# Grouped-query attention in a three-block network: the order of scores, turns, exponents and division on three engines

## The reference

```
def block_attention(q, k, v):
    ...
    scale = HEAD_DIM ** -0.5
    def attend(qblk):
        s = jnp.einsum('bqkgd,bskd->bkgqs', qblk, k, preferred_element_type=jnp.float32) * scale
        p = jax.nn.softmax(s, axis=-1).astype(v.dtype)
        return jnp.einsum('bkgqs,bskd->bqkgd', p, v)
```

## Time and profile before

| | us |
|---|---|
| median of 3 runs | 4406.19 (4401.25 to 4415.43) |
| the profiled execution | 4411.9 |
| its span, from the first instruction to the last | 4410.1 |
| its TensorE busy in the span | 3855.5 (87%) |
| its VectorE busy | 2755.7 (62%) |
| its ScalarE busy | 2025.5 (46%) |
| the attention phase in that span, first key copy to last store issued | 1302.6 to 1619.1 |

### The profile page before, as it was taken

The page is one execution under the profiler, slowest core; times in us unless marked ns, Lnnn a source line. Parts: engine busy times, 40 slices in busy tenths (PEclk is TensorE's granted clock), DMA queues, the critical chain, the costliest instruction groups (busy, mean ns, idle before and its releaser), DMA issues. The chain is left out here.

```text
span 4410.1 us, 51714 instructions
## 1 busy us (share of the span) xinstructions
PE 3855.5 (87%) x18779; PEld 3060.4 (69%) x18779; DVE 2755.7 (62%) x3345; ACT 2025.5 (46%) x2786; POOL 427.1 (10%) x322
## 2 busy tenths in 40 slices
PE   8998878799968878979669999999997998765979
PEld 6887836588727754967358888888885786644867
DVE  4336854654437765756579999999996334446442
ACT  3004641433326643143347777777774103453523
POOL 0000041140001221010001011010100400000020
PEclk9999989899979988989879999999997999887989
DMA  4325151223250025165469999999995223524441
GB/s 146 109 95 139 42 168 48 66 100 114 86 181 15 23 96 195 44 214 150 143 228 380 391 383 378 393 378 388 386 377 198 76 95 115 161 74 139 101 141 39
DMA packets 422643, 771.03 MB, mean 175 GB/s; under 512 B 106919, under 2 KB 249831, under 8 KB 420808
## 3 DMA queue, kind: packets, MB, share of 16 engines
q1 hardware_dynamic: 394648, 697.72, 45.2%
q10 hardware_dynamic: 23216, 54.27, 3.2%
q0 software_dynamic: 4608, 16.78, 1.5%
HBM read 647.31 MB, written 118.88 MB: 174 GB/s over the span
## 5 line engine op out<-in xcount | busy, mean ns | idle before, releaser
L4499 DVE TENSOR_TENSOR experts_w_lo<-b2e_ring,experts_w_hi 128x2048 fp32r<-128x2048 f32 x192 | 437.6, 2290 | 63.9 <-ACT experts_w_hi L4448 63.9
L4499 DVE TENSOR_TENSOR experts_w_lo<-top_xT,experts_w_hi 128x2048 fp32r<-128x2048 f32 x192 | 435.7, 2287 | 33.7 <-ACT experts_w_hi L4448 31.4
L4448 ACT ACTIVATE experts_w_hi<-b2e_ring 128x2048 fp32r<-128x2048 f32 x192 | 368.0, 1920 | 133.8 <-PE experts_gate L77 82.0
L4448 ACT ACTIVATE experts_w_hi<-top_xT 128x2048 fp32r<-128x2048 f32 x192 | 367.8, 1921 | 120.7 <-PE experts_up L77 65.6
L75 PE MATMUL experts_y_ps<-experts_w_hi,experts_act_hi 128*128 128x512 f32 x512 | 205.6, 401 | 0.0
L75 PE MATMUL experts_gate<-experts_w_hi,experts_xg_hi 128*128 128x512 f32 x512 | 201.9, 394 | 1.5 <-DVE experts_xg_lo L4505 1.5
L75 PE MATMUL experts_up<-experts_w_hi,experts_xg_hi 128*128 128x512 f32 x512 | 200.9, 392 | 0.0
L77 PE MATMUL experts_y_ps<-experts_w_hi,experts_act_lo 128*128 128x512 f32 x512 | 200.5, 392 | 0.0
L77 PE MATMUL experts_gate<-experts_w_hi,experts_xg_lo 128*128 128x512 f32 x512 | 200.2, 391 | 0.0
L76 PE MATMUL experts_gate<-experts_w_lo,experts_xg_hi 128*128 128x512 f32 x512 | 199.9, 390 | 0.0
L76 PE MATMUL experts_y_ps<-experts_w_lo,experts_act_hi 128*128 128x512 f32 x512 | 199.8, 390 | 0.0
(11 more groups left out here) (829 smaller groups left out, 10233.3 us busy)
## 6 DMA issues: line engine op xcount, KB each, us to landing
top_xT<-in_w_gate SPq DMA_DIRECT2D x128, 1024.0 KB, 7.1
b2e_ring<-in_w_up SPq DMA_DIRECT2D x128, 1024.0 KB, 8.6
top_xT<-in_w_down SPq DMA_DIRECT2D x64, 1024.0 KB, 9.2
b2e_ring<-in_w_down SPq DMA_DIRECT2D x64, 1024.0 KB, 8.6
proj<-b_in_out ACTq DMA_DIRECT2D x43, 512.0 KB, 2.7
b_in_w<-in_w_in SPq DMA_DIRECT2D x19, 1024.0 KB, 5.3
b_y<-in_w_in SPq DMA_DIRECT2D x28, 512.0 KB, 3.7
x_spill<-top_xT SPq DMA_DIRECT2D x3, 4096.0 KB, 15.5
```

Of the source, the lines that this page charges most:

```text
L4448: nc.scalar.activation(w_hi[n % HIS][:, :, :], ring[n % RING], ACT.Copy).then_inc(hi_ready, 1)
L4499: nc.vector.tensor_tensor(w_lo[n % HIS][:, :, :], ring[n % RING], w_hi[n % HIS][:, :, :].bitcast(F32), ALU.subtract).then_inc(lo_ready, 1)
```

## The change

The same instructions are issued, with the same semaphores and buffers; three lists get another order, and in the prologue one piece of scores and one maximum fewer are done ahead of the loop.

```
             pe.wait_ge(v_ready, 2 * NG * NV)
-            for j in range(2):
-                for n in range(NP):
-                    score(j, n)
+            for n in range(NP):
+                score(0, n)
+            for n in range(NP - 1):
+                score(1, n)
             for j in range(NT + 2):
-                if 1 <= j <= NT and NG > 2:
-                    turn(j - 1, 2)
+                if j + 1 < NT:
+                    score(j + 1, NP - 1)
+                if j < NT:
+                    for g in range(NG - 1):
+                        turn(j, g)
                 if j + 2 < NT:
-                    for n in range(min(2, NP)):
+                    for n in range(NP - 1):
                         score(j + 2, n)
-                if j < NT:
-                    for g in range(min(2, NG)):
-                        turn(j, g)
-                if j + 2 < NT and NP > 2:
-                    score(j + 2, 2)
                 if j >= 2:
                     product(j // 2 - 1, j % 2)
+                if j < NT:
+                    turn(j, NG - 1)
...
+                if j < NT:
+                    for g in range(NG - 1):
+                        split(j, g)
                 if j + 1 < NT:
                     exponent(j + 1)
                 if j < NT:
-                    for g in range(min(2, NG)):
-                        split(j, g)
+                    split(j, NG - 1)
                 if j >= 3 and j % 2 == 1:
                     lower_half(j // 2 - 1)
-                if j < NT and NG > 2:
-                    split(j, 2)
...
-            for j in range(2):
-                maximum(j)
-                join_maximum(j)
+            maximum(0)
+            join_maximum(0)
             for j in range(NT + 3):
-                leaving = j >= 4 and j % 2 == 0
                 for g in range(1, NKV):
                     if j == kv_step[g]:
                         split_k(g)
-                if leaving:
+                if j + 1 < NT:
+                    maximum(j + 1)
+                    join_maximum(j + 1)
+                if j >= 4 and j % 2 == 0:
                     join_halves(j // 2 - 2)
+                    divide(j // 2 - 2)
                 if j < NT:
+                    for g in range(NG - 1):
+                        split(j, g)
                     inverse(j)
-                if leaving:
-                    divide(j // 2 - 2)
-                if j + 2 < NT:
-                    maximum(j + 2)
-                if j < NT:
-                    split(j, 0)
-                if j + 2 < NT:
-                    join_maximum(j + 2)
-                if j < NT:
-                    for g in range(1, NG):
-                        split(j, g)
+                    split(j, NG - 1)
```

## The result

| | before | changed |
|---|---|---|
| median of 20 runs each, us | 4405.61 (4398.75 to 4415.43) | 4412.85 (4408.10 to 4422.84) |
| ratio, with its 95% interval | | 1.0018 (1.0012 to 1.0024) |
| span of the profiled execution | 4410.1 | 4407.9 |
| attention, first key copy to last store issued | 1302.64 to 1619.12: 316.5 | 1300.05 to 1624.16: 324.1 |

The changed kernel is 0.18% slower, 7 to 8 us: a small change, but with 20 runs each its interval lies clear of 1. The two profiled executions differ the other way, by 2.2 us, and must not be read as the result. The attention is 7.6 us longer in the second; TensorE's first matmul of the experts, whose code is the same, comes 4.9 us later there (2265.9 and 2270.8), and the remainder of the program, not touched by the change, happened to take 7.1 us less. Single executions of either kernel lie 15 to 17 us apart.

What follows compares the result with a forecast made beforehand. No engine was full; a 4.91 us ring of waits between TensorE and VectorE set the pace. Steady part +10.8 and start -4.1 gave +6.7 us on the 4406.2 median: 4413 us, range 4400 to 4426.

Steps and rivals of the forecast that it cites:

- wait of the maximum for scores: VectorE's maximum waiting for TensorE's scores, 30.2 us in 36 times in the old trace; claimed to go.
- odd unit, one run and two: Attention units without a division, between third lower parts: 3.96 us with the maximum in one run, 4.05 in two.
- even unit, one run and two: Attention units with the division, now behind the maximum: 5.38 us with the maximum in one run, 5.60 in two.
- new wait of TensorE for the division, one run: TensorE reaches an even unit's product at 1.92 us, the division ends at 2.66: a wait of 0.74 us.
- key split of unit 26: Unit splitting the second head's keys; ScalarE's copy and VectorE's split lie ahead of the maximum: 2.6 us extra.
- start: Attention up to unit 2: unit 0's turns no longer wait 1.71 us for two large score pieces; -4.1 us.
- The ring: Closed chain of waits across TensorE, VectorE and ScalarE, one third lower part to the next: 3.96 odd, 5.38 even.
- The two-run terms: Extra for units whose maximum is cut in two: 0.22 us in even units, 0.1 too late in odd ones.
- the falling clock: Rival: new waits let TensorE's clock fall to 1.2 GHz in the attention, giving 4560 us; chance 0.02.
- A hidden division: Rival: division done when TensorE reaches the product, even units 4.64 us, total 4388, 0.4% less; chance 0.07.
- ScalarE bound: Rival: the exponent ends late and delays odd units' third upper part; 4420 us at 0.6 late, 4429 at 0.9; chance 0.13.
- A clock below 1.00 in the steady part: Sign of being wrong: TensorE's granted clock under 1.00, that is 2.4 GHz, in the attention's regular units.

Runs made afterwards that it cites:

- the first run above: Changed kernel with VectorE joining and dividing ahead of the maximum in even units; ratio 0.9965 to the kernel before the change, median 4392.45 us.

## Why the prediction was right

It gave 4413 (4400 to 4426); measured are 4412.85, and 1.0018 of the kernel before. By its steps:

| step | predicted | in the trace |
|---|---|---|
| wait of the maximum for scores | gone | gone (30.2 to 0) |
| odd unit, one run and two | 3.96 and 4.05 | 3.93 and 4.08 |
| even unit, one run and two | 5.38 and 5.60 | 5.36 and 5.61 |
| new wait of TensorE for the division, one run | 0.74 in each of 30 | 0.73 to 0.74 by the starts of the matmuls (the rows themselves say 1.01 for the weight load, 0.59 for the matmul) |
| key split of unit 26 | 2.6 | 4.1 |
| units 2 to 62 | +10.8 | +11.8 |
| start | -4.1 | -4.1 |
| sum | +6.7 | +7.6 in the attention, +7.2 between the medians |

- **The ring.** The chain for even units was read off the end of the old trace, where the division stood without a maximum, plus the one row that goes between. It held to 0.02 us, and both moves of the division changed even units to within 0.1 of what the chain says while odd ones stayed, but for the units where the clock fell.
- **The two-run terms.** Estimates without a row (0.22 in even units, 0.1 in odd ones) measured 0.25 and 0.15.
- **The step that was mis-sized** is the key split in the sum: "I take 2.6, since nothing on VectorE overlaps them". The delay of the maximum was 2.6 (1435.55 + 0.34 to 1438.53), but the step counted that alone. Behind the wait that it causes the clock fell, which cost the other 1.5: 1.26 up to the third turn and 0.24 behind it. I had looked at the longest wait of a usual unit (0.74) when I gave the falling clock its small chance. The other units, odd ones with one run by 0.03 above all, came out 0.5 shorter together and gave part of it back.
- **The start.** Counted from the first key copy, as in the old trace, units 0, 1 and 2 come at 1322.05, 1325.63 and 1330.33; worked out were 1322.1, 1325.7 and 1330.3.
- **What was luck.** That 4413 meets the median to 0.2 us: single runs lie 15 us apart, and the stage itself came out 0.9 us longer than its sum, with two errors that partly cancel.
- **The rivals.** A hidden division needed the maximum out of its way; the first run above put it there and gave a ratio of 0.9965, where the rival said 4388, 0.4% less. ScalarE bound only the odd units with two runs, by 0.15. The clock fell in unit 26 alone (0.64 and 0.93 from 1440 to 1448). A clock below 1.00 in the steady part stood among the signs of being wrong: it came true for that one unit, and the ordinary units kept 1.00.

## What to carry to other kernels

Where three engines pass work round in their own fixed orders, pick one instruction per unit as a clock and add up start-to-start times along each closed chain of waits; the longest sets the pace, and a reordering is priced by what it puts into that chain. An instruction on whose result another engine waits (here joining and division, 0.9 us together) should not stand behind a long one that has slack: moving three lines turned 0.2% slower into 0.4% faster. Look once at the odd unit out, too: a rare long instruction in such a place can stall TensorE so that it loses its clock as well.

## What the runs showed of the hardware that was not expected

- Equal waits of TensorE left the clock alone or were followed by its fall. With the division moved back further, waits of 2.2 to 3.2 us went with a fall in six of the 29 even units other than unit 26, three of them among eleven waits of 2.47. With ScalarE's old list it was six of twelve waits of 2.0 us, and none of eighteen of 1.5 (1330 to 1680). What parts them is not settled by these runs.
- Ahead of the spreading matmuls TensorE's weight load stands idle 0.36 us with nothing to wait for (10.1 us in 28 units with the division first), but the matmul itself starts only 0.09 later than it could. Two waits on semaphores that are already met stand in front of it in the list and a third behind the first matmul; they may be the cause, which was not tried alone.
